# Up projections in seven block products, and another order of transfers and rows around the first expert

## The chip, the cores and the metric

One core of one Trainium2 chip runs the whole program. The metric is the device time of one execution in microseconds; of three executions of a kernel the median is taken. Everything is float32.

## The reference, cut to what matters

256 tokens of width 1024 pass through two layers of a first block and one layer of a second one. Each layer of the first block mixes tokens (a gated delta rule and a causal attention) and then runs a feed-forward part, `hid = causal_dwconv(x @ w_up, ffn_conv_w) + ffn_conv_b`, `gate, val = split(hid, 2)`, `ffn = (silu(gate) * val) @ w_down`, with a convolution of three taps over the tokens and a hidden width of 2816. The second block runs a differential and a dilated attention, and then 16 experts, of which each takes the 32 tokens with the highest affinity and computes `(silu(xe @ wg) * (xe @ wu)) @ wd` with weights of its own of 1024x2816, 1024x2816 and 2816x1024.

## The kernel before

The program writes out by hand, for each engine, its instructions in order and the semaphores between them. All weights stream through SyncE's one DMA queue. The names of engines in the rows are PE (TensorE), DVE (VectorE), ACT (ScalarE), POOL (GpSimd) and SP (SyncE).

**The feed-forward part of a layer.** The hidden channels are 22 tiles of 128 (`FT`). Tile `j` needs two outputs of 128 channels x 256 tokens, gate and value: `channels` (L608) makes them with 2 x 8 products of a 128x128 piece of the weights with 256 tokens, into one of four PSUM banks (`UP_BANKS`). For the first three tiles (`AHEAD`) the products are cut in two by tokens, 128 at a time, because the second half of the tokens comes out of the layer norm later. A float32 product is two instructions in the trace. ScalarE then takes the convolution's last tap out of the bank (L1423, two instructions a tile), VectorE adds the other two taps (L1886, four instructions), ScalarE takes the silu (L1428), and VectorE multiplies gate and value into `hidT` (L1894). PE waits for tile `j - 4`'s taps before it overwrites that bank. The weights come in units of 2 MB for two tiles each, in a ring of four.

The down projection behind it, `down_product` (L634), is already computed with seven block products for eight (Strassen's scheme in Winograd's form, over halves of tokens and output columns), of 512 columns each; VectorE forms its sums of weights and of hidden blocks in `down_sums` (L1869 to L1878), for the first two of the eleven pairs inside the tile loop, at `j` of 19 and 20, and for the others behind it.

**GpSimd** has little to do: three tensor operations a layer for the rotary embedding (L506 to L509), and DMAs of its own. In layer 0 it starts four copies of the bias table in DRAM (L515) while the up projections run, in layer 1 twelve loads behind the layer's last out product (L519 to L531).

**The second block and the first expert.** `attention` runs 16 steps on PE, with other work filled in by `second_fill`: at steps 15 and 16 the differential outputs are transposed (`diff_rows_transposed`, L1072), ScalarE copies them (`diff_mixed`, L1479), and their output projection (`diff_mix_half`, L1086) follows. SyncE may load `gate_up(0, 1)`, `gate_up(0, 3)` and `down(0, 1)` only when the last attention product (L729) has freed their place, so the experts' stream begins there. An expert is eight steps `k` of gate and up products (L1210), three transpositions (L1216) with their copies on ScalarE (L1499), and ten down chunks (L1229) that go through five buffers (`DOWN_CHUNKS`, the first of three rows of 128, the others of two) twice. Every step frees a buffer, for which SyncE waits with the next load: 2.8 MB for a gate and up step, 1.0 or 1.5 MB for a down chunk. Of the first expert five steps, both halves of step 5's gate (`gate_ahead`) and five down chunks are loaded before it starts; step 5's up half comes in two DMAs of 704 KB (L468) when step 0 has freed a buffer.

## Time and profile before

| | |
|---|---|
| median of 3 executions | 2255.62 us (2252.44 to 2256.43) |
| profiled execution, its own time | 2251.84 us |
| its span | 2250.0 us |
| PE, DVE, ACT, POOL busy | 79%, 25%, 14%, 1% of the span |
| DMA | 693.86 MB, mean 308 GB/s |
| mean granted TensorE clock | 0.871 of full speed |

The span is the time from the first to the last instruction in the trace; 1.84 us of the execution lie outside of it. Busy shares are averages over stages with different limits: up to about 946 us the program works on few weights with much arithmetic, and behind that it streams the weights of 16 experts.

### The profile page before, as it was taken

What the parts mean: (1) busy time and instruction counts of PE and PEld (TensorE: products, weight loads), DVE (VectorE), ACT (ScalarE), POOL (GpSimd) and SP (SyncE); (2) the same over time, 40 slices, a digit from 0 to 9 for tenths busy, and PEclk for the clock granted to TensorE, in tenths of its full rate; (3) what the DMA queues carried; (4) which work ended last, traced back from release to release, by engine and by line L of the source; (5) the groups of instructions that cost most, each with busy time, mean ns of one, the idle gap of its engine ahead of it and who ended that gap; (6) DMA issues with size and microseconds to landing.
All of it is one profiled execution on the core that took longest, in us unless ns stands there. A gap on an engine that the chain in (4) does not pass through costs nothing.

```text
span 2250.0 us, 29462 instructions
## 1 busy us (share of the span) xinstructions
PE 1784.6 (79%) x12314; PEld 971.0 (43%) x12314; DVE 552.9 (25%) x1290; ACT 308.8 (14%) x742; POOL 32.7 (1%) x42
## 2 busy tenths in 40 slices
PE   8999999999999999987666666666665665666665
PEld 7867885786788566432211221221121121122122
DVE  3444338444433744420100101010010010010101
ACT  3231110223211112310000000000000000000001
POOL 0010000001100000000000000000000000000000
PEclk9999999999999999988867777877777777887877
DMA  8234552623544365399999999999999999999998
GB/s 289 76 113 142 191 177 108 221 103 113 159 151 150 131 224 210 131 397 415 424 424 425 424 425 424 425 424 425 425 425 425 425 424 425 425 425 424 425 425 342
DMA packets 150153, 693.86 MB, mean 308 GB/s; under 512 B 15936, under 2 KB 65664, under 8 KB 96962
## 3 DMA queue, kind: packets, MB, share of 16 engines
q1 hardware_dynamic: 143922, 683.68, 75.5%
q0 software_dynamic: 6016, 9.04, 1.2%
q8 instruction: 51, 0.84, 0.1%
q10 hardware_dynamic: 144, 0.13, 0.0%
q14 instruction: 20, 0.16, 0.0%
HBM read 691.72 MB, written 4.22 MB: 309 GB/s over the span
## 4 chain that ended last, share of the span: by engine, by line
PE 54%; DMA 37%; SPq 4%; DVE 2%; issue 2%; ACT 1%; DVEq 0%; ACTq 0%
DMA arena<-in_w_up 35%; PE bank L608 16%; PE bank L1210 7%; PE bank L634 6%; PE bank L761 6%; PE bank L1229 5%; SPq L415 3%; PE bank L1059 1%; PE bank L756 1%; PE bank L968 1%; DVE arena L2052 1%; PE bank L1063 1%; PE bank L988 1%; DMA arena<-in_w_down 1%; PE bank L694 1%
## 5 line engine op out<-in xcount | busy, mean ns | idle before, releaser
L1210 PE MATMUL bank<-arena 128*32 128x512 f32 (+1 forms) x3072 | 467.3, 764 | 282.7 <-DMA arena<-in_w_up 250.4
L608 PE MATMUL bank<-arena 128*128 128x256 f32 (+1 forms) x2208 | 381.9, 335 | 4.0 <-DMA arena<-in_w_in 2.7
L1210 PEld LDWEIGHTS bank<-arena 128*32 128x32 f32 x3072 | 112.0, 137 | 627.9 <-DMA arena<-in_w_up 333.9
L608 PEld LDWEIGHTS bank<-arena 128*128 128x128 f32 x2208 | 345.7, 191 | 41.4 <-issue 3.9
L1229 PE MATMUL bank<-arena 128*32 128x256 f32 x2816 | 229.3, 478 | 113.3 <-DMA arena<-in_w_down 104.3
L2052 DVE TENSOR_TENSOR arena<-arena,bank 64x256 f32<-64x256 f32 x96 | 40.1, 418 | 707.4 <-ACT arena L1496 705.7
L1229 PEld LDWEIGHTS bank<-arena 128*32 128x32 f32 x2816 | 97.3, 134 | 241.0 <-DMA arena<-in_w_down 131.7
L761 PE MATMUL bank<-arena 128*128 128x256 f32 x576 | 138.6, 387 | 0.0
L634 PE MATMUL bank<-arena 128*128 128x512 f32 x308 | 132.7, 592 | 0.0
L1496 ACT ACTIVATE arena<-bank 64x512 f32<-64x512 f32 (+1 forms) x48 | 23.2, 549 | 749.6 <-PE bank L1210 749.6
L1886 DVE SCALAR_TENSOR_TENSOR arena<-bank,arena 128x254 f32<-128x254 f32 (+1 forms) x176 | 76.8, 478 | 184.3 <-ACT arena L1423 181.0
L761 PEld LDWEIGHTS bank<-arena 128*128 128x128 f32 x576 | 104.7, 189 | 18.9 <-issue 4.6
L634 PEld LDWEIGHTS bank<-arena 128*128 128x128 f32 x308 | 58.1, 189 | 72.6 <-issue 71.7
L1423 ACT ACTIVATE arena<-bank,arena 128x256 f32<-128x256 f32 x88 | 45.0, 562 | 232.8 <-PE bank L608 232.8
L1216 PE MATMUL bank<-arena 128*128 128x128 f32 x96 | 27.3, 378 | 36.8 <-DVE arena L2052 36.8
L1184 PE MATMUL bank<-arena 128*128 128x512 f32 x96 | 55.7, 663 | 0.0
L1503 ACT ACTIVATE arena<-bank 64x256 f32<-64x256 f32 x16 | 6.1, 379 | 283.5 <-PE bank L1229 283.5
L2027 DVE COPY arena<-bank 128x256 f32<-128x256 f32 x17 | 7.2, 426 | 149.3 <-PE bank L1175 149.3
L1530 DVE SCALAR_TENSOR_TENSOR arena<-bank,arena 128x256 f32<-128x256 f32 (+1 forms) x64 | 22.0, 386 | 83.3 <-PE bank L694 83.3
L2060 DVE TENSOR_TENSOR arena<-arena,bank 128x1024 f32<-128x1024 f32 x32 | 37.7, 1219 | 13.5 <-PE bank L1242 13.5
L2025 DVE COPY arena<-bank 128x2 f32<-128x2 f32 x17 | 2.7, 159 | 155.5 <-PE bank L1168 155.5
L1216 PEld LDWEIGHTS bank<-arena 128*128 128x128 f32 x96 | 11.8, 172 | 62.6 <-DVE arena L2052 62.6
(295 smaller groups left out, 1324.9 us busy)
## 6 DMA issues: line engine op xcount, KB each, us to landing
arena<-in_w_gate SPq DMA_DIRECT2D x127, 1408.0 KB, 20.3
arena<-in_w_up SPq DMA_DIRECT2D x127, 1408.0 KB, 23.3
arena<-in_w_down SPq DMA_DIRECT2D x144, 1024.0 KB, 17.6
arena<-in_w_down SPq DMA_DIRECT2D x32, 1536.0 KB, 13.4
arena<-in_w_up SPq DMA_DIRECT2D x44, 1024.0 KB, 7.7
arena<-in_w_in SPq DMA_DIRECT2D x40, 1024.0 KB, 8.6
arena<-in_w_out SPq DMA_DIRECT2D x12, 1024.0 KB, 6.0
arena<-in_w_down SPq DMA_DIRECT2D x12, 512.0 KB, 4.2
```

Of the source, the lines that this page charges most:

```text
L415: sp.dma_start(to_[:, n, :], a[w][0, ahead:][bass.ds(e, 1), k * P:(k + 1) * P, :].rearrange("o p n -> (o p) n")).then_inc(sem(f"gu_in{slot ...
L608: last = mm(ps[bank][:, j * S + lo:j * S + lo + n], w[:, k, c:c + P], xT[:, k, lo:lo + n], start=(k == 0), stop=(k == KT - 1))
L634: return mm(ps[PRODUCT_BANK[m]][:, :], left, right, start=(i == 0), stop=(i == KP - 1))
L761: last = mm(ps[bank][:, j * S:(j + 1) * S], slot(u, 512)[:, k, c:c + P], xT[:, k, :], start=(k == 0), stop=(k == KT - 1))
L1184: mm(ps[1][:, :], ident, normed_rows[:, 0, 0:512], start=True, stop=True)
L1210: last = mm(ps[b][32 * q:32 * q + 32, 0:n], expert_x[:, k, :], w, start=(k == 0), stop=(k == KT - 1))
L1216: last = tr(ps[HID_BANKS[b]][:, (m % 2) * P:(m % 2 + 1) * P], hidden[:, m, :], ident)
L1229: last = mm(ps[5][32 * q:32 * q + 32, 0:256], hidden_t[:, c0 // P + r, 32 * half:32 * half + 32], down_ring[b][:, r, 256 * q:256 * q + 256 ...
L1423: last = f(ff_conv[:, j % 3, gv, :], ps[UP_BANKS[j % 4]][:, gv * S:(gv + 1) * S], ACT.Identity, scale=conv_w[:, 136 + c:137 + c], bias=con ...
L1886: last = w.scalar_tensor_tensor(ff_conv[:, j % 3, gv, s:S], ps[UP_BANKS[j % 4]][:, gv * S:(gv + 1) * S - s], conv_w[:, 48 + c:49 + c], ff_ ...
L2052: last = w.tensor_mul(hidden[64 * odd:64 * odd + 64, 2 * b:2 * b + m, :], blocks(expert_gate[0:64, c0:c0 + n]), blocks(ps[b][64:P, 0:n]))
L2060: w.tensor_add(xs, xs, banks[:, 512 * OUT_BANK[t]:512 * OUT_BANK[t] + 2048].rearrange("p (q n) -> p q n", q=4)[:, :, 0:256]).then_inc(sem( ...
```

## The change

**Up projections.** From tile 3 on, each tile is computed by `up_block_products`: seven products over half of the contraction (4 x 128) with 128 tokens each, 28 in all, where there were 16 of 256 tokens. The sums of token blocks, `x_sums`, are made once a layer by VectorE. The sums of weight blocks are made for each tile by GpSimd in `up_sums`, four operations of 128x512 with three drains, into three buffers (`UP_RING`); PE waits for them ahead of its fourth product of the tile, and GpSimd for PE's tile `j - 3`. VectorE puts the seven products together in `up_summed` (six operations) into `up_blocks` in SBUF, from which ScalarE and VectorE then take the taps. A tile has two banks, so PE waits for `up_summed` of tile `j - 2`. In VectorE's loop the product of gate and value of tile `j - 1` now stands behind the sums of tile `j`, and `down_sums` at `j` of 17 and 19. In layer 0 the four bias copies stand between GpSimd's sums, in layer 1 the sums stand behind the twelve loads.

**Second attention.** Both transpositions of differential outputs move to the end of step 15 on PE, behind that step's attention product, and ScalarE's first copy of them ahead of its step 15.

**First expert.** Four pieces of step 5's up weights (0.9 MB of 1.4) are loaded ahead: one of 256 KB right behind the first `gate_ahead`, two of 192 KB behind the second, and one of 256 KB when the router's logits are done. What remains is one DMA of 512 KB. The first expert goes through its down buffers in the order 1, 2, 0, 3, 4, and SyncE reloads them in that order. Some semaphores are merged, and the products that only keep the clock up read `x` in place of `xT`.

```diff
 DOWN_CHUNKS = [(1024, 3), (0, 2), (256, 2), (512, 2), (768, 2)]
 D_RING, DOWNS = len(DOWN_CHUNKS), 2 * len(DOWN_CHUNKS)
-UP_BANKS = (0, 1, 4, 5)
+UP_BANKS = (0, 1, 4)
+PAIR_BANKS = {0: (4, 5), 1: (0, 1)}
+FIRST_PAIR_BANKS = (2, 3)
+UP_RING = 3
+UP_PLACE = {1: (0, 0), 2: (0, 1), 6: (0, 2), 5: (0, 3), 3: (1, 0), 7: (1, 1), 4: (1, 2)}
 SECOND_BANKS = (0, 1, 4, 5, 4, 5, 4, 5, 4, 5, 4, 5)
...
+def up_ahead(b, half):
+    c0, n = PIECES[b]
+    lo = half * HALF + c0
+    sp.dma_start(ahead_up[b, half], a["w_up_2"][0, 0, (EXTRA + 1) * P:(EXTRA + 2) * P, lo:lo + n]).then_inc(sem("gate_ahead_in"), 16)
...
 gate_ahead(1)
+up_ahead(0, 1)
...
 gate_ahead(0)
+up_ahead(2, 0)
+up_ahead(2, 1)
+sp.wait_ge(sem("logits"), T)
+up_ahead(0, 0)
...
-    for half in range(2):
-        cs = slice(half * HALF, half * HALF + HALF)
-        sp.dma_start(gate_up_ring[:, 0, 1, cs], a["w_up_2"][0, 0, k * P:(k + 1) * P, cs]).then_inc(sem("gu_in0"), 16)
+    c0, n = PIECES[1]
+    w_ = a["w_up_2"][0, 0, k * P:(k + 1) * P, :].rearrange("p (h n) -> p h n", n=HALF)[:, :, c0:c0 + n]
+    sp.dma_start(gate_up_ring[:, 0, 1, :].rearrange("p (h n) -> p h n", n=HALF)[:, :, c0:c0 + n], w_).then_inc(sem("gu_in0"), 32)
 stream_gate_up(1, range(0, 2))
-stream_down(0, range(D_RING, DOWNS))
+for i, b in enumerate(FIRST_ORDER):
+    sp.wait_ge(sem("down_free"), D_RING + i + 1)
+    down(0, D_RING + b)
 stream_gate_up(1, range(2, KT))
+sp.wait_ge(sem("down_free"), D_RING + FIRST_LAST)
 stream_down(1, range(D_RING))
...
+def up_sums(l, j):
+    u = U_UP + j // 2
+    r, first = u % RING, 16 if u % RING == 0 else 0
+    pool.wait_ge(sem(f"slot_in{r}"), l * (UNITS // RING * 32 - first) + 32 * (u // RING + 1) - first)
+    if j >= AHEAD + UP_RING:
+        pool.wait_ge(sem("up_product"), at(l, "up_product", j - UP_RING + 1))
+    w = slot(u, 512)
+    cv, cg = (slice(c, c + P) for c in (j % 2 * P, j % 2 * P + 2 * P))
+    s1, s2, s4 = (up_weight_sums[j % UP_RING][:, n] for n in range(3))
+    nc.gpsimd.tensor_tensor(s1, w[:, 0:4, cg], w[:, 4:8, cg], ALU.add)
+    pool.drain()
+    nc.gpsimd.tensor_tensor(s2, s1, w[:, 0:4, cv], ALU.subtract)
+    nc.gpsimd.tensor_tensor(w[:, 0:4, cg], w[:, 0:4, cv], w[:, 0:4, cg], ALU.subtract)
+    pool.drain()
+    nc.gpsimd.tensor_tensor(s4, w[:, 4:8, cv], s2, ALU.subtract)
+    pool.drain().then_inc(sem("up_sums"), 1)
...
+for j in range(AHEAD, FT):
+    if j in (6, 9, 12, 15):
+        hs = slice(j - 6, j - 3)
+        pool.wait_ge(sem("up_product"), j - 2)
+        pool.dma_start(scratch[hs, 2 * S:].rearrange("h (p n) -> h p n", p=P), scratch[hs, 0:2 * S].unsqueeze(1).broadcast_to([3, P, 2 * S])).then_inc(sem("bias_out"), 16)
+    up_sums(l, j)
...
+for j in range(AHEAD, FT):
+    up_sums(DEPTH - 1, j)
...
+def up_block_products(j):
+    w = slot(U_UP + j // 2, 512)
+    cv, cg = (slice(c, c + P) for c in (j % 2 * P, j % 2 * P + 2 * P))
+    s1, s2, s4 = (up_weight_sums[j % UP_RING][:, n] for n in range(3))
+    t1, t2, t3, t4 = (x_sums[:, n] for n in range(4))
+    left_right = {
+        1: (w[:, 0:4, cv], xT[:, 0:4, 0:P]),
+        2: (w[:, 4:8, cv], xT[:, 4:8, 0:P]),
+        3: (s4, xT[:, 4:8, P:S]),
+        4: (w[:, 4:8, cg], t4),
+        5: (s1, t1),
+        6: (s2, t2),
+        7: (w[:, 0:4, cg], t3),
+    }
+    pair = FIRST_PAIR_BANKS if j == AHEAD else PAIR_BANKS[j % 2]
+    for m in (1, 2, 4, 5, 6, 7, 3):
+        if m == 5:
+            pe.wait_ge(sem("up_sums"), at(l, "up_sums", j - AHEAD + 1))
+        left, right = left_right[m]
+        b, at_ = UP_PLACE[m]
+        for k in range(4):
+            last = mm(ps[pair[b]][:, at_ * P:(at_ + 1) * P], left[:, k, :], right[:, k, :], start=(k == 0), stop=(k == 3))
+    return last
...
+pe.wait_ge(sem("x1_copied"), at(l, "x1_copied", 5))
 for j in range(AHEAD, FT):
     if j % 2 == 0:
         unit_in(l, U_UP + j // 2)
-    if j >= 4:
-        pe.wait_ge(sem("up_convolved"), at(l, "up_convolved", j - 3))
-    up(j).then_inc(sem("up_product"), 1)
+    if AHEAD < j <= AHEAD + 2:
+        pe.wait_ge(sem("up_convolved"), at(l, "up_convolved", AHEAD if j == AHEAD + 1 else 2))
+    elif j > AHEAD + 2:
+        pe.wait_ge(sem("up_summed"), at(l, "up_summed", j - 2 - AHEAD + 1))
+    up_block_products(j).then_inc(sem("up_product"), 1)
...
-if i in (15, 16):
-    diff_rows_transposed(i - 15)
...
+def diff_outputs_transposed():
+    for t in range(T):
+        diff_rows_transposed(t)
+attention(L, SECOND_PAIRS, {i: lambda i=i: second_fill(i) for i in range(20)}, {15: diff_outputs_transposed})
...
-half, b = j // D_RING, j % D_RING
+half, b = j // D_RING, FIRST_ORDER[j % D_RING] if first else j % D_RING
...
+def hidden_silu(j):
+    act.wait_ge(sem("up_convolved"), at(l, "up_convolved", j + 1))
+    f(ff_conv[:, j % 3, 0, :], ff_conv[:, j % 3, 0, :], ACT.Silu).then_inc(sem("gate_silu"), 1)
+for j in range(FT):
+    if j > AHEAD:
+        hidden_silu(j - 1)
+    if j < AHEAD:
         act.wait_ge(sem("up_product"), at(l, "up_product", j + 1))
...
+    else:
+        act.wait_ge(sem("up_summed"), at(l, "up_summed", j - AHEAD + 1))
+        act.wait_ge(sem("hidden_ready"), at(l, "hidden_ready", j - 2))
+    for gv in range(2):
+        c = gv * FT + j
+        from_ = ps[UP_BANKS[j]][:, gv * S:(gv + 1) * S] if j < AHEAD else up_blocks[:, 2 * gv:2 * gv + 2, :].rearrange("p x y -> p (x y)")
+        last = f(ff_conv[:, j % 3, gv, :], from_, ACT.Identity, scale=conv_w[:, 136 + c:137 + c], bias=conv_w[:, 180 + c:181 + c])
+    last.then_inc(sem("up_last_tap"), 1)
+    if 0 < j <= AHEAD:
+        hidden_silu(j - 1)
+hidden_silu(FT - 1)
...
+| {i: lambda pi=pi: diff_squares(pi) for pi, i in enumerate((8, 9, 11))} | {13: diff_roots, 16: lambda: diff_mixed(1)},
+{15: lambda: diff_mixed(0)})
...
+t1, t2, t3, t4 = (x_sums[:, n] for n in range(4))
+(b11, b12), (b21, b22) = ((xT[:, k:k + 4, 0:P], xT[:, k:k + 4, P:S]) for k in (0, 4))
+v.drain()
+v.wait_ge(sem("x1_copied"), at(l, "x1_copied", 4))
+w.tensor_sub(t1, b12, b11)
+w.tensor_sub(t3, b22, b12)
+v.drain()
+w.tensor_sub(t2, b22, t1)
+v.drain()
+w.tensor_sub(t4, t2, b21).then_inc(sem("x1_copied"), 1)
+def block(pair, m, n=1):
+    b, at_ = UP_PLACE[m]
+    return ps[pair[b]][:, at_ * P:(at_ + n) * P].rearrange("p (x y) -> p x y", y=P)
+def up_summed(j):
+    pair = FIRST_PAIR_BANKS if j == AHEAD else PAIR_BANKS[j % 2]
+    v.wait_ge(sem("up_product"), at(l, "up_product", j + 1))
+    w.tensor_copy(up_blocks[:, 6:7, :], block(pair, 1))
+    v.drain()
+    w.tensor_tensor(up_blocks[:, 0:5:4, :], up_blocks[:, 6:7, :].broadcast_to([P, 2, P]), block(pair, 2, 2), ALU.add)
+    v.drain()
+    w.tensor_tensor(up_blocks[:, 5:6, :], up_blocks[:, 4:5, :], block(pair, 5), ALU.add)
+    w.tensor_tensor(up_blocks[:, 6:7, :], up_blocks[:, 4:5, :], block(pair, 7), ALU.add)
+    v.drain()
+    w.tensor_tensor(up_blocks[:, 1:4:2, :], up_blocks[:, 5:6, :].broadcast_to([P, 2, P]), block(pair, 3, 2), ALU.add)
+    w.tensor_tensor(up_blocks[:, 2:3, :], up_blocks[:, 6:7, :], block(pair, 4), ALU.subtract).then_inc(sem("up_summed"), 1)
+def hidden_product(j):
+    v.wait_ge(sem("gate_silu"), at(l, "gate_silu", j + 1))
+    w.tensor_mul(hidT[:, j, :], ff_conv[:, j % 3, 0, :], ff_conv[:, j % 3, 1, :]).then_inc(sem("hidden_ready"), 1)
+for j in range(FT):
+    if j >= AHEAD:
+        up_summed(j)
+    if j > AHEAD:
+        hidden_product(j - 1)
+    v.wait_ge(sem("up_last_tap"), at(l, "up_last_tap", j + 1))
+    for s in range(1, FTAPS):
+        for gv in range(2):
+            c = (2 - s) * 2 * FT + gv * FT + j
+            from_ = ps[UP_BANKS[j]][:, gv * S:(gv + 1) * S - s] if j < AHEAD else up_blocks[:, 2 * gv:2 * gv + 2, :].rearrange("p x y -> p (x y)")[:, 0:S - s]
+            last = w.scalar_tensor_tensor(ff_conv[:, j % 3, gv, s:S], from_, conv_w[:, 48 + c:49 + c], ff_conv[:, j % 3, gv, s:S], ALU.mult, ALU.add)
+        if s < FTAPS - 1:
+            v.drain()
+    last.then_inc(sem("up_convolved"), 1)
+    v.drain()
+    if 0 < j <= AHEAD:
+        hidden_product(j - 1)
+    if j in (17, 19):
         v.drain()
...
+        down_sums((j - 17) // 2)
+hidden_product(FT - 1)```

On PE in layer 0 the rows around tile 3 stood as follows before (`x47` ends the first three tiles, then come tiles 3 and 4; `slot_in` is a unit of weights, and rows that wait for something say for what).

```order
L608 MATMUL bank<-arena 128x128 [waits x1_copied]
L608 MATMUL bank<-arena 128x128 x47
L608 MATMUL bank<-arena 128x256 x16
L608 MATMUL bank<-arena 128x256 [waits up_convolved,slot_in0]
L608 MATMUL bank<-arena 128x256 x15
```

With the change they read:

```order
L656 MATMUL bank<-arena 128x128 [waits x1_copied]
L656 MATMUL bank<-arena 128x128 x47
L1078 MATMUL bank<-arena 128x128 [waits x1_copied]
L1078 MATMUL bank<-arena 128x128 x11
L1078 MATMUL bank<-arena 128x128 [waits up_sums]
L1078 MATMUL bank<-arena 128x128 x15
L1078 MATMUL bank<-arena 128x128 [waits up_convolved,slot_in0]
L1078 MATMUL bank<-arena 128x128 x11
```

A tile is 12 products, a wait for GpSimd's sums, and 16 products. Of VectorE's rows for a tile (here one in the middle of the loop) there were these:

```order
L1886 SCALAR_TENSOR_TENSOR arena<-bank,arena 128x255 [waits up_last_tap]
L1886 SCALAR_TENSOR_TENSOR arena<-bank,arena 128x255
L1886 SCALAR_TENSOR_TENSOR arena<-bank,arena 128x254 x2
L1894 TENSOR_TENSOR arena<-arena 128x256 [waits gate_silu]
```

They are now these, where `arena` is SBUF and `bank` is PSUM; the taps' input has moved from the one to the other:

```order
L1994 COPY arena<-bank 128x128 [waits up_product]
L1996 TENSOR_TENSOR arena<-arena,bank 128x2x128
L1998 TENSOR_TENSOR arena<-arena,bank 128x128
L1999 TENSOR_TENSOR arena<-arena,bank 128x128
L2001 TENSOR_TENSOR arena<-arena,bank 128x2x128
L2002 TENSOR_TENSOR arena<-arena,bank 128x128
L2007 TENSOR_TENSOR arena<-arena 128x256 [waits gate_silu]
L2019 SCALAR_TENSOR_TENSOR arena<-arena 128x255 [waits up_last_tap]
L2019 SCALAR_TENSOR_TENSOR arena<-arena 128x255
L2019 SCALAR_TENSOR_TENSOR arena<-arena 128x254 x2
```

On GpSimd, where nothing stood between them before, the rows around tile 6 in layer 0 are one of the four bias copies and the sums of a tile:

```order
L560 DMA bias_rows<-bias_rows 3x128x512 [waits up_product]
L535 TENSOR_TENSOR arena<-arena 128x512 [waits up_product,slot_in1]
L537 TENSOR_TENSOR arena<-arena 128x512
L538 TENSOR_TENSOR arena<-arena 128x4x128
L540 TENSOR_TENSOR arena<-arena 128x512
```

The copy now waits ahead of each third tile's sums in one queue.

## Rows read from the trace of the kernel before

**Rows 1.** Page, 40 slices: granted clock and DMA share in tenths.
```profile
PEclk9999999999999999988867777877777777887877
DMA  8234552623544365399999999999999999999998
```

**Rows 2.** Chain that ended last, in order of time: start us, us, what.
```profile
200.54 145.97 PE bank L608 x736
413.48 7.14 PE bank L608 x64
600.52 145.97 PE bank L608 x736
```

**Rows 3.** Timeline, last tiles of layer 0's up projections: start, us, engine, line, operation.
```profile
339.62 1.02 ACT L1423 ACTIVATE arena<-bank,arena 128x256 f32<-128x256 f32 x2 [5.60 <-PE bank L608]
340.68 1.82 DVE L1886 SCALAR_TENSOR_TENSOR arena<-bank,arena 128x255 f32<-128x255 f32 x4 [0.87 <-ACT arena L1423]
342.94 0.43 DVE L1894 TENSOR_TENSOR arena<-arena 128x256 f32<-128x256 f32 x1 [0.44 <-issue]
343.46 0.69 DVE L1869 TENSOR_TENSOR arena<-arena 128x512 f32<-128x512 f32 x1
```

**Rows 4.** Timeline: VectorE's operations with one input in PSUM.
```profile
110.83 1.12 DVE L1811 SCALAR_TENSOR_TENSOR arena<-arena,bank 128x128 f32<-128x128 f32 x4 [2.15 <-PE bank L935]
112.14 0.42 DVE L1821 TENSOR_TENSOR arena<-arena,bank 128x256 f32<-128x256 f32 x1 [0.19 <-issue]
```

**Rows 5.** Timeline of GpSimd: tensor operations, and DMA starts in both layers.
```profile
113.88 1.99 POOL L506 TENSOR_TENSOR arena<-arena 128x1024 f32<-128x1024 f32 x1 [91.19 <-DVE arena L1825]
...
118.47 2.36 POOL L509 TENSOR_TENSOR arena<-arena 128x1024 f32<-128x1024 f32 x1 [0.64 <-issue]
222.42 1.18 POOL L515 DMA_DIRECT2D bias_rows<-bias_rows  x1 [101.59 <-PE bank L608]
...
592.81 0.62 POOL L519 DMA_DIRECT2D arena<-in_norm_g  x1 [72.16 <-PE bank L988]
...
599.12 0.55 POOL L531 DMA_DIRECT2D arena<-in_norm_columns  x1
```

**Rows 6.** Timeline around steps 15 and 16 of the second attention.
```profile
924.77 0.63 PE L1072 MATMUL bank<-arena 128*128 128x128 f32 x4 [1.89 <-DVE arena L1948]
...
928.13 0.57 ACT L1479 ACTIVATE arena<-bank 128x512 f32<-128x512 f32 x1
...
928.85 3.72 PE L1086 MATMUL bank<-arena 128*128 128x512 f32 x8
```

**Rows 7.** Stretches: us, busy PE PEld DVE ACT POOL, PEclk, DMA share, GB/s.
```profile
924.00:928.00 4.00, 3.23 (x17) 1.82 (x18) 3.71 (x13) 3.66 (x10) 0.00 (x0) 0.69 0.84 352
...
976.00:980.00 4.00, 3.48 (x33) 1.38 (x37) 1.72 (x7) 1.52 (x2) 0.00 (x0) 1.00 0.79 324
980.00:984.00 4.00, 4.00 (x44) 1.32 (x40) 0.00 (x0) 0.00 (x0) 0.00 (x0) 1.00 0.78 255
...
1012.00:1016.00 4.00, 4.00 (x60) 2.07 (x56) 0.00 (x0) 0.00 (x0) 0.00 (x0) 0.71 0.72 239
...
2100.00:2200.00 100.00, 62.97 (x490) 19.02 (x490) 6.85 (x15) 4.65 (x9) 0.00 (x0) 0.77 1.01 425
```

**Rows 8.** Timeline of SyncE's DMA starts around the first expert.
```profile
946.04 0.33 SPq L415 DMA_DIRECT2D arena<-in_w_gate  x1
...
979.88 0.81 SPq L468 DMA_DIRECT2D arena<-in_w_up  x2
982.25 0.33 SPq L415 DMA_DIRECT2D arena<-in_w_gate  x1
...
1012.27 4.88 SPq L423 DMA_DIRECT2D arena<-in_w_down  x5
```

**Rows 9.** Timeline: the first expert's last transposition, and its down products.
```profile
1008.26 0.69 PE L1216 MATMUL bank<-arena 128*128 128x128 f32 x2 [0.18 <-DVE arena L2052]
...
1009.42 7.33 PE L1229 MATMUL bank<-arena 128*32 128x256 f32 x88 [0.47 <-ACT arena L1499]
```

97 lines of the change are left out of this document (39 added, 58 removed).

## The prediction

> **What bounds the kernel now.** I read the slices first. DMA is between a fifth and four fifths busy in the first 17 of 40 slices, and full in nearly all from the eighteenth on, while the granted clock of TensorE is full before and falls behind [rows 1]. A late stretch of 100 us moves 425 GB/s at a DMA share of 1.01 [rows 7]. So there are two programs: up to 946 us, where SyncE starts the experts' stream [rows 8], the chain of work runs on PE, and behind that it is the number of bytes. Whatever PE saves before 946 us starts the stream earlier and comes off the end in full. What PE saves behind it is worth only the holes in the stream that it closes.
>
> The chain shows PE without a break in the up projections: 736 instructions in 145.97 us in layer 0 and the same in layer 1 [rows 2]. The other engines fit beside it: for a tile ScalarE takes 1.02 us, VectorE 1.82 and 0.43 [rows 3].
>
> **Up projections, PE.** A product is two instructions. The 736 are 64 products of 128 tokens and 19 x 16 = 304 of 256. In the same code 64 instructions of 128 tokens take 7.14 us [rows 2], 0.2231 us a product. The 64 make 14.28 us, which leaves 131.69 us for 19 tiles, 6.93 each. A tile of the change is 28 x 0.2231 = 6.25 us. Saved: 19 x 0.684 = 13.0 us a layer.
>
> **Up projections, VectorE.** The sums are one copy and three operations of 128x128 and two of 128x256 with an input in PSUM. Rows of that kind are 1.12 / 4 = 0.28 and 0.42 us [rows 4]: 4 x 0.28 + 2 x 0.42 = 1.96, and with drains I take 2.3. A tile is then 2.3, ScalarE's 1.02 (the 0.43 product lies beside it), the taps' 1.82 and some 0.2 between them: 5.3 us, under PE's 6.25. At tiles 17 and 19 a `down_sums` comes on top. Its operations are four pairs of 0.69 and 0.28 us; with drains the first pair of them starts at 343.46 and I take 3.6 us for all [rows 3]. VectorE is 2.65 us late after tile 17, catches up 0.95, and is 4.35 late after tile 19. PE bears 6.25 - 2.3 = 3.95. I charge 0.9 us a layer for this and for the first waits of the down product. The four sums of tokens (4 x 0.69 = 2.8 us) are done some 10 us before PE needs them, 14.28 us behind 200.54. If that cover were gone they would cost 2.8 us.
>
> **Up projections, GpSimd.** Its rows show 1024 elements in 1.99 and 2.36 us, and 0.64 us of idle time over a drain [rows 5]. An operation of 512 is then 1.0 to 1.18 us, a tile with three drains 5.7 to 6.6 us. I take 6.6, since the 2.36 is the one add without a repeated input. That is over PE's 6.25, but GpSimd has a start: it is free at 192.8 in layer 0 (the same wait ends at 592.81 in layer 1, and the loads end at 599.7 [rows 5]), and PE's tile 3 begins at 200.54 + 14.28 = 214.8. Tile 6's sums may start when PE ends tile 3, so they are ready 6.25 + 6.6 = 12.9 us behind its start. PE needs them after three tiles and 12 products, at 21.4. The spare is 8.6 us, and 15 tiles use 15 x 0.35 = 5.3 of it. In layer 0 four DMA starts of 1.1 to 1.18 us use 4.5 more, which leaves about 1 us uncovered. So GpSimd costs 0 to 1 us, if it runs undisturbed. Both layers: 2 x (13.0 - 0.9) = 24.2 us.
>
> A tensor operation on GpSimd is the least certain price. The Trainium skill (GPSIMD Engine Reference, Elementwise — side-by-side cycle accounting) has 4497 ns for an add of 2048 float32; halved twice, as an estimate, that is 1.12 us for 512, inside the bounds above, and the sum would stay.
>
> **Second attention.** PE idles 1.89 us for VectorE's scaled outputs before the first transposition at 924.77, and its attention product of step 15 stands behind that. ScalarE copies the outputs at 928.13, behind its exponentials, and the output projection starts at 928.85 [rows 6]. In the new order the attention product fills the idle time, both transpositions end near 927, the copy follows at once, and the projection starts near 927.2: 1.6 us earlier. The clock was 0.69 in that stretch [rows 7]; less idling may return a little, and I take 2.0 in all, from 0 (ScalarE's exponentials delayed instead) to 3.5. It shifts 946 us, so it counts in full.
>
> **First expert.** A hole costs the bytes that are missing against 425 GB/s. From 976 to 984 us that is 4 x (425 - 324) / 425 + 4 x (425 - 255) / 425 = 2.55 us, from 1012 to 1016 us 4 x (425 - 239) / 425 = 1.75 us [rows 7]. For the first: SyncE can start nothing until step 0 ends at 979.88 [rows 8]. 640 KB more in the queue cover 1.5 us of it, and 256 KB more go out when the stream is idle (0.6 us). But then the 979.88 DMA carries only 512 KB, 1.2 us, and the next start is at 982.25 [rows 8], so about 1.1 us of hole comes back. Net 1.0 us. For the second: down products start at 1009.42, behind ScalarE's last copy, and SyncE's first reload is at 1012.27 [rows 8, 9], after a chunk of three rows, 24 instructions. With a chunk of two rows that needs only the first piece, PE starts at about 1008.95 and frees it after two thirds of 2.85 us, at 1010.85: 1.4 us earlier. Part two is worth 2.0 + 1.0 + 1.4 = 4.4 us, from 0 to 7.
>
> **The sum.** 24.2 + 4.4 = 28.6 us off the profiled execution's 2251.84 (span 2250.0 and 1.84 around it) gives 2223.2. The median of the runs stands 3.8 above that execution, so the forecast is 2255.6 - 28.6 = 2227.
>
> **Rival one, slower: VectorE and GpSimd in each other's way.** The taps now read both inputs from SBUF, as the product does, and so does GpSimd. No row shows the two at once: beside GpSimd's operations VectorE ran such with an input in PSUM [rows 4, 5], and neither was stretched. Suppose an operation of one keeps the other's waiting to its end. A tile then needs 1.82 + 0.43 = 2.25 us of VectorE and 4 x 1.18 = 4.7 of GpSimd in turn, 7.0 against 6.25. GpSimd's chain becomes 6.6 + 0.8 = 7.4 us, its spare 7.8, gone after seven tiles, and the last nine lose 1.15 each, 10 us. VectorE's eight operations of each `down_sums` wait up to 1.18 each, which costs about 8 more a layer beyond what PE bears. A layer loses: 13.0 - 10 - 8, less 0.6 for the first waits, is -5.6 us, and layer 0's DMA starts 4.5: 2255.6 + 11.2 + 4.5 - 4.4 = 2267. It decides from a pace of 7.3 us a tile. For it speaks that the two loads fill more than a tile's time; against it that nothing here shows such waiting. The Trainium skill states this very rule (SBUF — State Buffer, Who interferes with whom): a VectorE instruction with two SBUF inputs and a GpSimd instruction that reads SBUF exclude one another for the whole instruction. By that rule the time is this rival's or the next one's; since no run here shows it, I don't give it more than half.
>
> **Rival two: the same, with short operations.** At 1.0 us GpSimd's chain is 6.7 and stays inside its spare; only VectorE at tiles 17 and 19 is late, by 4 to 9 us a layer. That leaves 6.5 a layer: 2255.6 - 13 - 4.4 = 2238.
>
> **Rival three: GpSimd alone is slower than its rows.** Inputs in pieces of 128 or slow wake-ups give 7.2 us a tile, a spare of 8.0 against 15 x 0.95 = 14.3: a layer gains 13.0 - 0.9 - 6.3 = 5.8, less 4.5 in layer 0. 2255.6 - 7.1 - 4.4 = 2244. That the seven products don't pay on PE at all is excluded by the 7.14 us row, whose products change their weights each time too.
>
> **How the numbers follow.** Forecast 0.44, rival one 0.32, rival two 0.15, rival three 0.09. The forecast's own range is 2220 to 2235 (part two from 0 to 7, up to 4 of lateness). Rival one alone reaches from 2251 to 2290. A range of 2219 to 2270 leaves out 0.16 of it above and 0.04 below. A change within 0.2% (4.5 us) can't be told from none: rival one gives 0.07 of that and two 0.02. Faster 0.66, same 0.09, slower 0.25.
>
> **What would show it.** Right: PE's chain over the up projections is 14.3 + 119 us with no idle time ahead of the fourth product of a tile; the taps still take 1.82 us and a GpSimd operation at most 1.2; the first reload of a down buffer is closer to the first expert's last gate and up product. Wrong: taps above 2.5 us where GpSimd is busy, PE waiting for GpSimd or for `up_summed` from the tenth tile on, worst at tiles 18 to 21; or holes of the same size in the stream around steps 0 and 5 of the first expert.

## The result, and the profile after

| | before | after |
|---|---|---|
| median of the runs (us) | 2255.62 (2252.44 to 2256.43) | 2315.38 (2313.38 to 2318.43) |
| ratio, 95% interval | | 1.0275 (1.0264 to 1.0287) |
| span of the profiled execution (us) | 2250.0 | 2313.6 |
| mean granted clock | 0.871 | 0.859 |

The change makes the kernel 60 us slower: the medians, each of five executions, differ by 59.8 us, the ratio in the table corresponds to 62, and the profiled executions differ by 63.5. The forecast was 2227, the range ended at 2270, and the slower rival said 2267: all three are too low. In the rows below L535 to L541 are GpSimd's four sums and the three drains between and behind them (a drain is the instruction by which the program lets an engine wait for its own earlier work), L560 is its bias copy, L1078 are PE's block products, L1994 to L2002 VectorE's sums of blocks, L2007 its hidden product, L2019 its taps, L1517 ScalarE's last tap.

First where the time is lost. This is the chain of waits of the changed kernel, in order of time (start us, us, what), next to [rows 2].

```profile
651.35 14.29 PE bank L656 x128
810.12 66.31 PE bank L682 x154
887.57 21.23 PE bank L656 x160
```

Layer 1's up projections begin at 651.35 where they began at 600.52: 50.8 us lost in layer 0. The down product behind them begins at 810.12 where it was 746.49: 12.8 more. What follows keeps that distance, and the span is 63.6 longer. So all is lost in the two up stages, and layer 0 loses four times what layer 1 does. What PE waited for, layer 0's stage first, then layer 1's (what, us in total, times, longest):

```profile
PE bank L1078 <- POOLq L541: 42.4, 4, 13.1
PE bank L1078 <- DVE arena L2002: 8.7, 2, 7.8
...
PE bank L1078 <- DVE arena L2002: 18.4, 14, 4.9
```

Two different causes, then: PE waits for the drain that signals GpSimd's sums, four times in layer 0, and for VectorE's sums of blocks in layer 1. GpSimd's timeline at the first of the four, next to [rows 5]:

```profile
222.12 1.17 POOL L560 DMA_DIRECT2D bias_rows<-bias_rows  x1 [10.13 <-PE bank L1078]
223.32 1.29 POOL L535 TENSOR_TENSOR arena<-arena 128x512 f32<-128x512 f32 x1
240.73 1.26 POOL L537 TENSOR_TENSOR arena<-arena 128x512 f32<-128x512 f32 x1 [16.12 <-issue]
241.95 1.27 POOL L538 TENSOR_TENSOR arena<-arena 128x512 f32<-128x512 f32 x1
...
244.87 1.28 POOL L535 TENSOR_TENSOR arena<-arena 128x512 f32<-128x512 f32 x1 [0.24 <-issue]
246.28 1.28 POOL L537 TENSOR_TENSOR arena<-arena 128x512 f32<-128x512 f32 x1
```

Between a tile's first and second sum there is one drain. At 246.28 it leaves hardly a gap; at 240.73, behind a DMA start, there are 16.12 us, put down to no other engine ("issue"). The four DMA starts as a group (ns shortest, median, longest, first and last start), and layer 0's second sums by line (busy us, mean ns, idle before):

```profile
L560 POOL DMA_DIRECT2D bias_rows<-bias_rows x4: 1082/1100/1173, 222.1 to 320.4; - x4
...
DMA to landing us min/median/max: 14.6/17.2/18.4
```

```profile
L537 POOL TENSOR_TENSOR arena<-arena 128x512 f32<-128x512 f32 x18 | 23.2, 1288 | 60.5 <-issue 58.5
```

The longest landing ends at 222.12 + 18.4 = 240.5, and the second sum starts at 240.73. The other three transfers land at 273.7, 304.3 and 337.9, and the second sums behind them start at 273.81, 304.50 and 338.09. The four idle times are 58.5 us together.

Now VectorE in layer 1: groups by line and form (busy us, mean ns of one, idle before), and the taps of one tile in layer 0 and of one in layer 1 with GpSimd's sums beside them.

```profile
L2019 DVE SCALAR_TENSOR_TENSOR arena<-arena 128x255 f32<-128x255 f32 x36 | 38.6, 1113 | 9.3 <-ACT arena L1517 9.0
L2019 DVE SCALAR_TENSOR_TENSOR arena<-arena 128x254 f32<-128x254 f32 x36 | 31.9, 924 | 1.3
L2007 DVE TENSOR_TENSOR arena<-arena 128x256 f32<-128x256 f32 x20 | 16.0, 802 | 0.3
L1996 DVE TENSOR_TENSOR arena<-arena,bank 128x256 f32<-128x256 f32 x18 | 7.6, 422 | 1.3
```

```profile
262.77 1.83 DVE L2019 SCALAR_TENSOR_TENSOR arena<-arena 128x255 f32<-128x255 f32 x4 [0.83 <-ACT arena L1517]
...
708.66 4.73 DVE L2019 SCALAR_TENSOR_TENSOR arena<-arena 128x255 f32<-128x255 f32 x4 [0.83 <-ACT arena L1517]
708.90 1.37 POOL L535 TENSOR_TENSOR arena<-arena 128x512 f32<-128x512 f32 x1 [4.77 <-PE bank L1078]
710.42 1.27 POOL L537 TENSOR_TENSOR arena<-arena 128x512 f32<-128x512 f32 x1
711.65 1.46 POOL L538 TENSOR_TENSOR arena<-arena 128x512 f32<-128x512 f32 x1
713.25 1.28 POOL L540 TENSOR_TENSOR arena<-arena 128x512 f32<-128x512 f32 x1
```

The four taps take 1.83 us at 262.77, where GpSimd stands in its long drain, and 4.73 at 708.66, beside three of GpSimd's sums and the start of a fourth. VectorE's operations with one input in a bank keep their 0.42 us. This is rival one's mechanism, but it isn't GpSimd's chain that sets the pace, as rival one had it: beside the taps GpSimd's operations grow by 0.1 to 0.2 us and it waits for PE (4.77 us at 708.90); VectorE's tile becomes some 7.5 us, and PE waits for that. GpSimd is not spared everywhere, though. Ahead of layer 0's up projections a sum of its own meets VectorE's longer operations of the layer norm, both inputs in SBUF, and both grow:

```profile
195.91 1.94 DVE L1740 SCALAR_TENSOR_TENSOR arena<-arena 128x1024 f32<-128x1024 f32 x1
196.90 2.07 POOL L540 TENSOR_TENSOR arena<-arena 128x512 f32<-128x512 f32 x1
```

Apart from each other the first takes 1.28 us (at 646.55) and the second 1.28 (at 244.87).

The stream behind 1009 us, in stretches as in [rows 7], and SyncE's starts as in [rows 8]:

```profile
1044.00:1048.00 4.00, 4.00 (x44) 1.30 (x40) 0.00 (x0) 0.00 (x0) 0.00 (x0) 1.00 0.57 153
1048.00:1052.00 4.00, 4.00 (x48) 1.33 (x44) 0.00 (x0) 0.00 (x0) 0.00 (x0) 1.00 0.89 310
1076.00:1080.00 4.00, 4.00 (x76) 2.23 (x68) 0.00 (x0) 0.00 (x0) 0.00 (x0) 0.97 0.94 328
```

```profile
1009.31 0.33 SPq L427 DMA_DIRECT2D arena<-in_w_gate  x1
...
1044.25 0.62 SPq L490 DMA_DIRECT2D arena<-in_w_up  x1
```

The first hole is 4 x (272 + 115) / 425 = 3.6 us, where it was 2.55, the second 0.9 instead of 1.75. The stream starts 63.27 us late (1009.31 for 946.04) where the up stage ended 63.63 late. By these three numbers part two is worth next to nothing here: 0.4 us in the second attention and 0.9 at the second hole, against 1.1 lost at the first.

### The profile page after: what moved, and what is told of

Its sections match the earlier page's. It is cut to its first block, busy times and chain, and to the rows that moved or that the text cites. A ratio compares the mean times of both kernels' runs of the same rounds, so it can differ in the third digit from the quotient of the medians.

```text
span 2313.6 us, 31944 instructions
## 1 busy us (share of the span) xinstructions
PE 1776.6 (77%) x13226; PEld 992.4 (43%) x13226; DVE 702.9 (30%) x1526; ACT 315.5 (14%) x742; POOL 232.3 (10%) x194
## 4 chain that ended last, share of the span: by engine, by line
PE 41%; DMA 37%; DVE 6%; issue 5%; SPq 4%; POOLq 2%; DVEq 2%; ACT 2%; POOL 1%; ACTq 0%
DMA arena<-in_w_up 36%; PE bank L1293 6%; PE bank L811 6%; PE bank L682 6%; PE bank L1312 5%; PE bank L656 4%; SPq L427 3%; DVE arena L2019 2%; PE bank L1078 2%; PE bank L1137 1%; PE bank L806 1%; PE bank L1018 1%; DVE arena L2184 1%; PE bank L1141 1%; PE bank L1038 1%
## 5 line engine op out<-in xcount | busy, mean ns | idle before, releaser
L1078 PE MATMUL bank<-arena 128*128 128x128 f32 x2128 | 256.6, 284 | 69.5 <-POOLq L541 42.4
L1078 PEld LDWEIGHTS bank<-arena 128*128 128x128 f32 x2128 | 252.9, 200 | 73.0 <-POOLq L541 43.2
L2019 DVE SCALAR_TENSOR_TENSOR arena<-arena 128x254 f32<-128x254 f32 (+1 forms) x152 | 127.8, 881 | 25.0 <-ACT arena L1517 21.9
L682 PE MATMUL bank<-arena 128*128 128x512 f32 x308 | 133.2, 592 | 0.2 <-DMA arena<-in_w_down 0.2
L1590 ACT ACTIVATE arena<-bank 64x512 f32<-64x512 f32 (+1 forms) x48 | 23.2, 549 | 754.2 <-PE bank L1293 754.2
L656 PE MATMUL bank<-arena 128*128 128x128 f32 (+1 forms) x992 | 118.9, 282 | 4.1 <-DMA arena<-in_w_in 2.7
L656 PEld LDWEIGHTS bank<-arena 128*128 128x128 f32 x992 | 116.6, 195 | 7.9 <-issue 3.9
L811 PEld LDWEIGHTS bank<-arena 128*128 128x128 f32 x576 | 104.7, 189 | 18.9 <-issue 4.6
L682 PEld LDWEIGHTS bank<-arena 128*128 128x128 f32 x308 | 57.8, 189 | 73.4 <-issue 70.8
L1517 ACT ACTIVATE arena<-arena 128x256 f32<-128x256 f32 x76 | 41.5, 594 | 146.7 <-DVE arena L2002 146.7
L535 POOL TENSOR_TENSOR arena<-arena 128x512 f32<-128x512 f32 x38 | 50.0, 1315 | 100.3 <-PE bank L1038 71.8
L537 POOL TENSOR_TENSOR arena<-arena 128x512 f32<-128x512 f32 x38 | 48.7, 1281 | 71.3 <-issue 66.7
L1299 PE MATMUL bank<-arena 128*128 128x128 f32 x96 | 26.2, 365 | 37.2 <-DVE arena L2184 37.2
L538 POOL TENSOR_TENSOR arena<-arena 128x512 f32<-128x512 f32 x38 | 52.9, 1392 | 0.0
```

The costliest lines, as they stand in the source:

```text
L535: nc.gpsimd.tensor_tensor(s1, w[:, 0:4, cg], w[:, 4:8, cg], ALU.add)
L538: nc.gpsimd.tensor_tensor(w[:, 0:4, cg], w[:, 0:4, cv], w[:, 0:4, cg], ALU.subtract)
L656: last = mm(ps[bank][:, j * S + lo:j * S + lo + n], w[:, k, c:c + P], xT[:, k, lo:lo + n], start=(k == 0), stop=(k == KT - 1))
L682: return mm(ps[PRODUCT_BANK[m]][:, :], left, right, start=(i == 0), stop=(i == KP - 1))
L811: last = mm(ps[bank][:, j * S:(j + 1) * S], slot(u, 512)[:, k, c:c + P], xT[:, k, :], start=(k == 0), stop=(k == KT - 1))
L1078: last = mm(ps[pair[b]][:, at_ * P:(at_ + 1) * P], left[:, k, :], right[:, k, :], start=(k == 0), stop=(k == 3))
```

## The experiments

Twelve kernels. The medians of the kernel before beside them were 2252.8 to 2253.2 us, so ratios are compared, not times with 2255.6.

| run | us | ratio to before (95%) |
|---|---|---|
| A. DMA starts behind the sums | 2273.51 | 1.0090 (1.0073 to 1.0107) |
| B. waits for drains | 2278.34 | 1.0110 (1.0093 to 1.0127) |
| C. A, taps read a PSUM bank | 2238.67 | 0.9934 (0.9917 to 0.9950) |
| D. A without GpSimd's sums | 2226.79 | 0.9881 (0.9864 to 0.9897) |
| E. part two alone | 2251.09 | 0.9990 (0.9981 to 0.9999) |
| F. second attention alone | 2252.72 | 0.9998 (0.9989 to 1.0007) |
| G. A, convolution in PSUM | 2237.84 | 0.9931 (0.9917 to 0.9945) |
| H. G, down sums at 19 and 20 | 2236.96 | 0.9923 (0.9909 to 0.9936) |
| I. G, down sums at 18 and 21 | 2227.44 | 0.9880 (0.9863 to 0.9896) |
| J. I without part two | 2229.75 | 0.9895 (0.9878 to 0.9912) |
| K. I with the DMA starts back | 2278.82 | 1.0113 (1.0096 to 1.0130) |
| L. K with waits for drains | 2225.26 | 0.9877 (0.9861 to 0.9894) |

### The stall: runs A and B

**A.** The change with GpSimd's DMA starts moved.

```diff
                     for j in range(AHEAD, FT):
-                        if j in (6, 9, 12, 15):
-                            hs = slice(j - 6, j - 3)
-                            pool.wait_ge(sem("up_product"), j - 2)
-                            pool.dma_start(scratch[hs, 2 * S:]...)
                         up_sums(l, j)
+                    for n in range(4):
+                        hs = slice(3 * n, 3 * n + 3)
+                        pool.dma_start(scratch[hs, 2 * S:]...)
...
             pool.wait_ge(sem("rows_used"), DEPTH * ROW_UNITS + 1)
+            for j in range(AHEAD, FT):
+                up_sums(DEPTH - 1, j)
             pool.dma_start(gain, a["norm1_g_2"].broadcast_to([P, D])).then_inc(sem("gain_in"), 16)
...
-            for j in range(AHEAD, FT):
-                up_sums(DEPTH - 1, j)
```

> The changed kernel with GpSimd's DMA starts taken out from between its sums: layer 0's four bias copies come behind all its sums, and layer 1's sums come ahead of the twelve loads that the second attention needs. Nothing else differs. Theory (two causes): a drain of GpSimd that follows a DMA start waits until that transfer has landed, which costs 58.5 us of idle time in layer 0 and 8.2 in layer 1; what is left is VectorE made slow by GpSimd's sums. Then no idle time above 1 us stands at a first drain of the sums, and layer 0's up projections, now 196.6 us, last as long as layer 1's, some 155 to 160 us, 9 to 14 more than before in each layer: 2268 to 2280 us. Rival (one cause): the stalls only happen where GpSimd is late anyway, or the transfers slow VectorE and PE themselves wherever they are; then the 50 us of layer 0 stay nearly whole: 2305 to 2316 us.

2273.5 us, inside the theory's range. Layer 0's stage now costs about what layer 1's does: its up projections start at 200.82, those of layer 1 at 611.17, which is 10.4 us more than before for the whole stretch, and 11.2 more to the second attention. By the ratios (1.0275 and 1.0090), moving the DMA starts gave back 42 of the 62 us.

**B.** The change with its DMA starts in place, and no drain between the sums.

```diff
-                nc.gpsimd.tensor_tensor(s1, w[:, 0:4, cg], w[:, 4:8, cg], ALU.add)
-                pool.drain()
+                n = 3 * (l * (FT - AHEAD) + j - AHEAD)
+                nc.gpsimd.tensor_tensor(s1, ..., ALU.add).then_inc(sem("sums_own"), 1)
+                pool.wait_ge(sem("sums_own"), n + 1)
...
-                pool.drain()
+                pool.wait_ge(sem("sums_own"), n + 3)
-                nc.gpsimd.tensor_tensor(s4, w[:, 4:8, cv], s2, ALU.subtract)
-                pool.drain().then_inc(sem("up_sums"), 1)
+                nc.gpsimd.tensor_tensor(s4, ..., ALU.subtract).then_inc(sem("up_sums"), 1)
```

> The changed kernel with every DMA start where the change put it; only the three drains between and behind the four sums are replaced by waits on a semaphore of GpSimd's own that the sums count up. Theory: it is the drain that waits for the landing of a transfer that was started before it; with waits that count the sums alone the idle times of 12 to 16 us go, and layer 0 lasts as long as layer 1: 2268 to 2280 us. Rival: GpSimd itself (its descriptors, its port) can't work on tensors while its transfer is under way; then the four idle times stay between the DMA start and the second sum, and the time stays at 2305 to 2316 us.

2278.3 us, inside the theory's range. GpSimd's timeline at the same place (its lines are one further down here):

```profile
222.38 1.17 POOL L560 DMA_DIRECT2D bias_rows<-bias_rows  x1 [10.26 <-PE bank L1078]
223.57 1.29 POOL L536 TENSOR_TENSOR arena<-arena 128x512 f32<-128x512 f32 x1
224.94 1.27 POOL L538 TENSOR_TENSOR arena<-arena 128x512 f32<-128x512 f32 x1
226.18 1.46 POOL L539 TENSOR_TENSOR arena<-arena 128x512 f32<-128x512 f32 x1
```

The second sum starts 1.37 us behind the first, while the transfer is under way (13.5 to 18.1 us from start to landing in this layer). So neither GpSimd nor the transfer keeps the sums from running: it is the drain that waits for the landing. The 4.8 us by which the run is slower than A are lost in layer 0: from the start of its up projections to that of layer 1's there are 415.3 us where A has 410.4, and from there to the second attention they have 234.3 and 234.4. In layer 0 VectorE's taps take 1281 ns in B and 1121 in A, in layer 1 1109 in both. So it isn't the waits as such, which layer 1 has too; why the taps meet more of GpSimd's sums where the DMA starts stand between them was not tried.

### VectorE beside GpSimd: runs C and D

**C.** Run A with another input for the taps. What it computes is not the convolution of tiles 3 to 19.

```diff
-                            from_ = ps[UP_BANKS[j]][...] if j < AHEAD else up_blocks[...]
+                            from_ = ps[UP_BANKS[j] if j < AHEAD else 7][...] if j < 20 else up_blocks[...]
```

> The kernel of the run with the DMA starts behind the sums, in which the taps of tiles 3 to 19 read a PSUM bank instead of the summed blocks in SBUF (so their values are not the convolution's; every operation keeps its size and its waits). GpSimd's sums and the hidden product stay. Theory: VectorE's instruction with both inputs in SBUF and GpSimd's instruction exclude each other; the four taps of a tile take 1.8 to 2.0 us again beside GpSimd's sums, PE no longer waits for the summed blocks but at the last tiles, a tile takes 6.25 to 6.5 us, and the time is 2228 to 2245 us. Rival: the sums slow VectorE whatever it reads, or VectorE is late for its waits on ScalarE and not for its taps; then the taps or the gaps between them keep the tile at 7.4 us and the time stays within 5 us of the run with the DMA starts behind the sums.

**D.** Run A without the four sums of `up_sums` (one drain stays to signal).

> The kernel of the run with the DMA starts behind the sums, with GpSimd's four sums of weights left out for every tile (the waits and one drain stay, the products are of weights that nobody summed). Theory: PE's 28 products take 6.25 us a tile as the 7.14 us of 64 instructions say, VectorE's taps take 1.83 us, and each layer's up projections last 133 to 137 us against 146 before: 2226 to 2236 us. Rival: seven products with weights in blocks, or the sums on VectorE and the waits on ScalarE, don't keep 6.25 us even alone; then each layer stays at 146 us or above and the time at 2250 to 2280 us.

C takes 2238.7 and D 2226.8 us. The taps and the hidden product in layer 0's stage, by line and form: first of A, then of C, then of D.

```profile
L2018 DVE SCALAR_TENSOR_TENSOR arena<-arena 128x255 f32<-128x255 f32 x34 | 36.8, 1121 | 8.5 <-ACT arena L1516 8.5
L2006 DVE TENSOR_TENSOR arena<-arena 128x256 f32<-128x256 f32 x18 | 14.3, 796 | 0.2
```

```profile
L2018 DVE SCALAR_TENSOR_TENSOR arena<-bank,arena 128x255 f32<-128x255 f32 x36 | 15.7, 478 | 5.6 <-ACT arena L1516 4.0
L2006 DVE TENSOR_TENSOR arena<-arena 128x256 f32<-128x256 f32 x22 | 19.7, 895 | 0.8 <-ACT arena L1503 0.5
```

```profile
L2012 DVE SCALAR_TENSOR_TENSOR arena<-arena 128x255 f32<-128x255 f32 x38 | 16.7, 482 | 16.0 <-ACT arena L1510 16.0
L2000 DVE TENSOR_TENSOR arena<-arena 128x256 f32<-128x256 f32 x21 | 8.8, 420 | 0.7 <-ACT arena L1497 0.5
```

C leaves PE one wait of 3.1 us in layer 0's stage and one of 3.4 in layer 1's; A had 17.2 and 18.6 us of such waits. Two things must come together. With both inputs in SBUF and GpSimd at work a tap takes 1121 ns; take either away and it is 478 or 482. The hidden product, which C left in SBUF, stays long there (895) and is short only in D (420). The Trainium skill's rule (SBUF — State Buffer, Who interferes with whom) names this pair of conditions, and also that an instruction with at most one SBUF input is left alone, outside of modes that use two ports. The trace agrees on both: 478 ns with one input in SBUF, 1121 with two. D also shows that PE's price of the prediction held: 840 instructions, fifteen tiles, in 93.81 us, 6.25 each.

### Part two: runs E and F

> The kernel before with the change's second part alone: the order of the last steps of the second attention, the six rows loaded ahead for the first expert, and the first expert's order of down chunks and reloads. Forecast of the prediction: 4.4 us less (2.0 in the second attention, 1.0 and 1.4 in the two holes of the stream), a ratio of 0.998. Theory after the trace of the changed kernel: about 0.5 us in the second attention and nothing in the holes, since there the stream started 63.27 us late where the up projections ended 63.63 late, and the first hole had 3.6 us where 2.55 were before; 0 to 1 us less, a ratio of 0.9995 to 1.0. Rival: the holes of the changed kernel looked that way only because all stood 63 us later against the clock; then the 4.4 us show here.

> The kernel before with the new order of the last steps of the second attention alone (both transpositions of VectorE's outputs behind the attention product of step 15, ScalarE's first copy ahead of its exponentials). Forecast of the prediction: 2.0 us less, the output projection 1.6 us earlier behind the same attention product. Theory after the trace of the changed kernel: 0.4 to 0.6 us less. Rival: ScalarE's exponentials, delayed by the copy, take it all back, and nothing is left.

E has the hunks of the diff for the second attention and the first expert, F those of the second attention only. F measures 0.5 us less, which can't be told from none (from 2.5 less to 1.6 more), and E 2.1 us less (0.2 to 4.3). The interval of F alone doesn't exclude the forecast 2.0, so the traces have to say where it went. Stretches of before, then of F, then of E (as in [rows 7]: the last three numbers are the granted clock, the DMA share and GB/s):

```profile
964.00:968.00 4.00, 3.93 (x21) 2.64 (x22) 2.99 (x13) 2.38 (x6) 0.54 (x1) 0.81 0.95 389
...
976.00:988.00 12.00, 11.48 (x113) 4.02 (x117) 1.72 (x7) 1.52 (x2) 0.00 (x0) 1.00 0.87 339
...
1008.00:1020.00 12.00, 9.73 (x115) 4.89 (x118) 0.36 (x2) 1.16 (x3) 0.00 (x0) 0.74 0.90 354
```

```profile
964.00:968.00 4.00, 4.00 (x14) 2.64 (x14) 1.49 (x7) 1.06 (x5) 0.54 (x1) 0.50 1.03 428
...
976.00:988.00 12.00, 11.48 (x118) 4.13 (x117) 1.72 (x7) 1.67 (x2) 0.00 (x0) 1.00 0.71 273
```

```profile
976.00:988.00 12.00, 11.48 (x118) 4.16 (x114) 1.73 (x7) 1.67 (x2) 0.00 (x0) 1.00 0.80 290
...
1008.00:1020.00 12.00, 10.21 (x143) 5.49 (x142) 0.58 (x2) 0.77 (x2) 0.00 (x0) 0.86 0.99 400
```

In F the output projection starts at 927.56 instead of 928.85 and the stream at 944.70 instead of 946.04: 1.3 us earlier, so the first step did most of what it should. But between them and the expert TensorE's granted clock is 0.50 in a stretch where it was 0.81 (0.50 in E too), and the first product comes at 977.63 where it was 977.25. The stream's next start waits for the first expert's step 0, and goes out at 980.27 instead of 979.88. Its hole is 12 x (425 - 273) / 425 = 4.3 us against 2.4: longer by 1.9, about the 1.3 that it started earlier and the 0.4 that it goes on later. The gain became a hole. E's extra rows shorten that to 12 x (425 - 290) / 425 = 3.8, half a microsecond of the forecast 1.0; the second hole shrinks from 2.0 to 0.7 us, 1.3 of the forecast 1.4, and SyncE's first reload goes out at 1009.78 instead of 1012.27, 2.5 us earlier where 1.4 were forecast. E's theory, 0 to 1 us, lies under the 2.1 measured, though inside their interval: it had left out the second hole, which did shrink in the changed kernel as well.

### Toward a version that gains: runs G, H and I

**G.** Run A with the convolution's sums in three banks that are free in this stage. A tap then reads one input from PSUM and one from SBUF, and so does the hidden product.

```diff
+CONV_BANKS, CONV_TILES = (6, 7, 2), range(4, 19)
...
+        def ff(j, gv):
+            return ps[CONV_BANKS[j % 3]][:, gv * S:(gv + 1) * S] if j in CONV_TILES else ff_conv[:, j % 3, gv, :]
...
+                    if i == 0:
+                        pe.wait_ge(sem("hidden_ready"), at(l, "hidden_ready", 19))
                     product(1, i)
...
-                    f(ff_conv[:, j % 3, 0, :], ff_conv[:, j % 3, 0, :], ACT.Silu).then_inc(sem("gate_silu"), 1)
+                    f(ff_conv[:, j % 3, 0, :], ff(j, 0), ACT.Silu).then_inc(sem("gate_silu"), 1)
...
-                    w.tensor_mul(hidT[:, j, :], ff_conv[:, j % 3, 0, :], ff_conv[:, j % 3, 1, :])
+                    w.tensor_mul(hidT[:, j, :], ff_conv[:, j % 3, 0, :], ff(j, 1))
...
-                            last = w.scalar_tensor_tensor(ff_conv[:, j % 3, gv, s:S], from_, ..., ff_conv[:, j % 3, gv, s:S], ...)
+                            last = w.scalar_tensor_tensor(ff(j, gv)[:, s:S], from_, ..., ff(j, gv)[:, s:S], ...)
```

> The kernel of the run with the DMA starts behind the sums, with the convolution's sums of tiles 4 to 18 held in three PSUM banks that are free in that stage, so that each tap and each hidden product of VectorE reads one input from PSUM and one from SBUF; the last three tiles and the rest are as they were. The whole computation is done. Theory of VectorE and GpSimd excluding each other where VectorE's two inputs are in SBUF: the taps take 1.8 to 2.0 us a tile beside GpSimd's sums, the hidden product 0.45, a tile 6.25 to 6.4 us; what stays is the down sums of the last tiles, so the time lies a little under the run whose taps read a PSUM bank (2238.7) and over the run without sums (2226.8): 2228 to 2238 us. Rival: writing to PSUM is slow, or ScalarE and VectorE meet in the banks; then taps and activations are longer than 0.48 and 0.5 us each and the time is 2240 to 2275 us.

2237.8 us, inside the theory's range. What remains against D is the end of the stage, 4 to 5 us a layer. `down_sums` behind tile 17, whose inputs are all in SBUF, lasts 8.0 us beside GpSimd's last sums, which grow too, to 1.74 us. PE waits 2.8 us for that, and its next 112 instructions take 14.37 us instead of 12.5, with a granted clock of 0.61 from 324 to 328 us.

**H.** G with the two `down_sums` behind tiles 19 and 20.

> The run before this one, with the first two down sums behind tiles 19 and 20 instead of 17 and 19. The whole computation is done. Theory: GpSimd's last sums end while PE is on tile 19, so the down sums, whose inputs are all in SBUF, run undisturbed there, 0.69 us for an operation where they take 1.04 beside GpSimd; 0 to 4 us less than the run before this one in both layers together, toward the 2226.8 of the run without sums. Rival: they are then late for the down product, which waits for the first of them; 2 to 8 us more.

2237.0 us, 0.9 under G, which the two intervals don't tell apart. The down sums are short there (0.70 us for an operation of 512), but they stand ahead of the last sums of blocks: PE waits 2.8 us for these, and has a lower clock just behind that wait:

```profile
336.00:340.00 4.00, 2.16 (x6) 0.61 (x4) 3.70 (x12) 0.00 (x0) 0.00 (x0) 1.00 0.96 389
340.00:344.00 4.00, 3.05 (x4) 1.48 (x5) 2.92 (x9) 1.17 (x3) 0.00 (x0) 0.63 0.89 351
```

**I.** G (its banks now from tile 3 on) with the first `down_sums` behind tile 18 and the second between the last blocks and the last taps.

```diff
-                    if j in (17, 19):
-                        v.drain()
-                        down_sums((j - 17) // 2)
+                    if j == 18:
+                        v.drain()
+                        down_sums(0)
...
+                    if j == FT - 1:
+                        v.drain()
+                        down_sums(1)
                     v.wait_ge(sem("up_last_tap"), at(l, "up_last_tap", j + 1))
```

> The kernel with the convolution's sums in PSUM (now of tiles 3 to 18), with the first down sum behind tile 18 and the second behind the blocks of the last tile, ahead of its taps. The whole computation is done. Theory: in the run with both down sums behind tiles 19 and 20 PE waited 2.8 us for the last summed blocks and then ran its first down products at half clock, 4.0 us a layer in all against the run without sums; with the second one moved behind the last blocks it is still in time for the second pair of the down product (6.0 us a pair), so both losses go: 2228 to 2232 us, with 2226.8 for the run without sums. Rival: behind tile 18 the first down sum still meets GpSimd's sums for tile 21 and is stretched to 6 us or more, and the loss only moves: 2234 to 2239 us.

2227.4 us, ratio 0.988, just under the theory's range. PE waits for nothing in either up stage. Its chain, and the taps of layer 0 by form:

```profile
201.47 14.29 PE bank L660 x128
334.58 64.57 PE bank L686 x150
589.29 14.29 PE bank L660 x128
722.39 66.19 PE bank L686 x154
799.73 21.23 PE bank L660 x160
```

```profile
L2028 DVE SCALAR_TENSOR_TENSOR bank<-arena,bank 128x255 f32<-128x255 f32 x32 | 14.1, 486 | 13.1 <-ACT bank L1523 13.1
```

Each up stage lasts 133.1 us, 14.29 + 19 x 6.25, where it was 145.97 [rows 2]: 12.9 us, for the prediction's 13.0.

### The parts again in the fast version: runs J, K and L

> The run with down sums behind tiles 18 and 21, without the change's second part: the second attention's last steps and the first expert's loads and order are those of the kernel before. Theory: the part is worth what it is worth alone, where the ratio was 0.999 (2.1 us, interval 0.2 to 4.3): 2228 to 2231 us. Rival: with the up projections fast the stream starts elsewhere against TensorE's clock and the part is worth nothing or costs: 2225 to 2228 us.

> The run with down sums behind tiles 18 and 21, with GpSimd's DMA starts back where the change has them, between the sums of layer 0 and ahead of those of layer 1. Theory: with VectorE out of the way the first drain behind each start still waits for the landing, 12 to 16 us four times in layer 0 and 8 once in layer 1; GpSimd's spare absorbs about 8 of each layer's, so layer 0 is some 45 to 52 us longer and layer 1 0 to 2: 2270 to 2282 us. Rival: the stall was so long only because GpSimd was late already; with a pace of 5.8 us a tile against PE's 6.25 most of it is hidden: 2230 to 2250 us.

> The run before this one (DMA starts in the change's places), with the three drains of the sums replaced by waits on a semaphore that the sums themselves count up. Theory: no wait for a landing is left, the starts cost GpSimd their own 1.1 us each and the waits nothing more than the drains did: 2227 to 2231 us. Rival: the transfer itself holds GpSimd, or the 4.8 us by which waits were slower than moved starts before come back: 2232 us or more.

J is 2229.75 us: 0.15% above I, as E is 0.1% below before, though the two intervals overlap, so the rival is not excluded. K is I but for the place of the DMA starts, and L differs from K in the drains alone: 2278.8 against 2225.3, 53.6 us, all of it in layer 0 (the up projections of layer 1 start at 642.27 and 588.89). In K the idle time at the second sum is back as it was in the changed kernel, and in L it is gone; layer 0's groups, K first:

```profile
L542 POOL TENSOR_TENSOR arena<-arena 128x512 f32<-128x512 f32 x18 | 23.2, 1287 | 60.6 <-issue 58.6
```

```profile
L543 POOL TENSOR_TENSOR arena<-arena 128x512 f32<-128x512 f32 x18 | 23.3, 1295 | 1.4
```

L can't be told from I. So the stall needed no help from VectorE's lateness, and the drain is the whole of it. In L, where VectorE's taps keep their 0.49 us, waits with the DMA starts in place cost nothing against moved starts, where in B they cost 4.8 us; B and L differ in VectorE's operands and in the place of the two down sums.

## Why the prediction was wrong

**The step that failed** is the one on GpSimd: "In layer 0 four DMA starts of 1.1 to 1.18 us use 4.5 more, which leaves about 1 us uncovered. So GpSimd costs 0 to 1 us, if it runs undisturbed." The starts were priced by their own rows, and each start's duration was right (1.08 to 1.17). What was put at nothing is that the drain behind such a start waits for the landing, 14.6 to 18.4 us. The four waits are 58.5 us of idle time, against a spare of 8.6. That cost 42 us (changed kernel against A) and 53.6 (K against L). The rows read of before hold no GpSimd drain behind a DMA start that is still under way, so they couldn't show the wait. But the trace of before has the landing times of these same four copies, 13.8 to 17.5 us, and a wait of unknown scope behind a DMA start should have been bounded by them. With what it did cost, 42 to 54 us, on top of rival one's 2267 the sum is 2309 to 2321, and the measured time lies in it.

**The second part of that step**, "if it runs undisturbed", was weighed as rival one, and it decided as well: A is 20.6 us slower than before, where D is 26.1 faster. So the contention is 46.7 us with the down sums where the change put them. Rival one had the mechanism and its sign, taps above 2.5 us (4.73 at 708.66). Its pace, 7.4 us a tile where some 7.5 were found, is right in part by luck: its sum let GpSimd's operations wait for VectorE's, while beside the taps GpSimd's 1.27 us grow to at most 1.46 and VectorE's 0.48 us tap becomes 1.1. What the prediction held against this rival was only that before never had the two together, which is no evidence.

Either cause alone would have been enough to leave the range's end, 2270, behind: A (contention without the stall) has a ratio of 1.0090 and K (the stall nearly without contention) 1.0113, 2276 and 2281 us by the 2255.6 of before.

**What held.** PE's tile: 6.25 us. VectorE's sums of blocks: 0.28 to 0.42 each. `down_sums` undisturbed: 3.63 us in I (321.35 to 324.98) for the 3.6 taken. GpSimd's pace, by luck: the parts were off in opposite directions (1.27 to 1.46 us an operation instead of 1.0 to 1.18, and 0.14 to 0.24 a drain instead of 0.64), and the sum is 5.5 to 5.8 us. The prediction's 5.7 to 6.6 should have started at 5.9, by its own 4 x 1.0 + 3 x 0.64, so the tile is faster than its rows said. The sum for the two up stages, 24.2 us: in D layer 1's up projections start at 588.07 instead of 600.52, and the second attention's projections at 799.59 instead of 823.72, 24.1 us earlier, of which 0.5 were there before the up projections began (200.06 for 200.54). The four sums of tokens were taken at 2.8 us; in layer 0, beside GpSimd, they last 6.3 (201.94 to 208.2), which the cover of some 10 us hid. Rivals two and three fell: neither short operations nor a slow GpSimd was the case.

**Part two**, forecast at 4.4 us, is worth 2.1 (0.2 to 4.3). Its first term (2.0) is about zero by F's trace, given back as a longer hole in the stream; its second (1.0) is about 0.5, its third (1.4) about 1.3. The step that failed there is "It shifts 946 us, so it counts in full": the stream's next start hangs on the first expert's step 0, and that did not come earlier.

## What to carry to other kernels

Before an engine's idle time is filled with work, list what that work will share: the memory in which its neighbour's operands lie, and every instruction (a drain above all) that waits for more than the work it guards. Wait for the operation, not for the engine: a counted semaphore in place of a drain was worth 53.6 us here without moving anything. And where VectorE must run beside GpSimd, give its instructions one operand in PSUM: that turned 1.1 us taps back into 0.49 us ones. With the two down sums moved as well, these two make of a ratio of 1.0275 one of 0.988.

## What the runs showed of the hardware that was not expected

- A drain on GpSimd behind a DMA start returned only when the transfer had landed: 16.12 us of idle time at a landing of 18.4, and 8.17 at one of 9.4 in layer 1. A wait on a semaphore in the same place returned in under 0.1 us.
- When VectorE's instructions with two SBUF inputs met GpSimd's sums, the short ones lost far more than GpSimd's: a tap went from 482 to 1121 ns, a sum of 512 elements beside it from about 1.27 us to at most 1.46. Beside longer ones GpSimd lost as much: 2.07 us next to an operation of 1024 elements, which itself took 1.94 instead of 1.28.
- In both runs with the new order in the second attention (E and F) TensorE's granted clock was 0.50 from 964 to 968 us, where it had been 0.81, and the gain of 1.0 and 1.3 us at the stream's start was gone at the first expert's first product (977.74 and 977.63 for 977.25). PE had no more idle time than before in that stretch (busy 4.00 of 4.00 us, for 3.93); which earlier stretch the lower clock answers to was not tried.
